# One split pass of 96 rows for the input products of a state-space scan on TensorE

## The chip, the cores and the metric

One core of a Trainium2 chip runs the program. The metric is the device time of one execution in microseconds; the profile is of one execution and counts from its first instruction. TensorE is called PE in the rows, VectorE DVE, ScalarE ACT, GpSimd POOL and SyncE SP.

## The reference

Two blocks follow each other on 256 tokens of width 2048. The first has two layers, each with mixing (two attentions and a gating), attention over a memory, and a gated feed-forward of width 5632. The second block runs once: sliding-window attention beside a state-space branch, both gated, merged and projected. All is float32. What the change touches is the start of the state-space branch. `u` (256 tokens x 1024) is cut into 64 groups of 16 features, and every group has 64 complex states:

```
bu_re = einsum('blgh,gph->blgp', u, B_re)
bu_im = einsum('blgh,gph->blgp', u, B_im)
b_re, b_im = cf * (bu_re + i bu_im)          # a factor per state, folded into C in the kernel
s[t] = a * s[t-1] + b[t]                     # complex, along the 256 tokens
y = einsum(s_re, C_re) - einsum(s_im, C_im) + D_skip * u
```

## The kernel before

**Weights and their split.** All large weights come as one stream of 512 KB units, 1032 in all, two 128-row blocks by 512 columns each. SP loads a unit into one of four slots (L644). ScalarE rounds it to fp32r (`hi`, L1149), VectorE writes the rest (`lo = raw - hi`, L1708), and TensorE multiplies hi by xh, lo by xh and hi by xl (L677 to L679 in form "T", 12 matmuls with 512 columns; L685, L687, L688 in form "C", 24 matmuls with 256 columns). An fp32r matmul takes one pass; the three products together stand for a float32 one. A slot is free when its unit has been multiplied, so the hi split of a unit waits for TensorE to finish the unit four before it, and the splits run three units ahead at most.

**Order of work.** Every engine has one instruction queue, in the order of the code. In the second block that order is one list, `SMIX`, made by `second_steps()`: all units of the weight stream in turn, and between them the other steps, each with a position in units. Every engine walks through the same list and does its own part of each step; ScalarE and VectorE split three units ahead of the unit that the list has reached. So a step at position 28.5 stands on TensorE between units 28 and 29, and on ScalarE between the hi splits of units 31 and 32. In this block u0 and u1 are units 0 to 15, ag0 and ag1 16 to 31, then ga0, ap0, ga1, ap1 and so on; units 80 to 95 (z0, z1) are of form C, as are 0 to 31. Window attention (steps wL, wE, wT, wV) lies at positions 6 to 24.

**The scan.** The 64 groups are worked in 8 chunks (`c`) of 8 groups, that is 128 features and 4 x 128 states. Chunk c begins at position 26.5 + 12.2 c:
- `inputs` re and im (L1074 to L1083, TensorE, positions +0 and +1): four matmuls each, recorded as two instructions a matmul, with a 128x128 block of `bpad` as weights and `uT[:, c, :]` (128 features x 256 tokens) as the moving side, both plain float32, into PSUM. `bpad` holds B of the chunk placed block-diagonally, zeros in between.
- `back` 0 to 5 (L2419 to L2435, VectorE, from +0.6): a rotation that turns the complex recurrence into a real one. back 0 waits for re, back 2 for im.
- `scan` (L2443, VectorE, from +4.2): eight scans of 256 tokens.
- `forward` 0 to 5 (L2452 to L2463, VectorE, from +6.8): the rotation back. After it the states are ready (L2464).
- `outputs` (L1092, TensorE, +11.9): 8 plain float32 matmuls of the states with `cpad`. `skip` (L2475, VectorE, +12.9) adds u.
- `turns` (L1651 to L1664, ScalarE, +12.6 for chunk c + 2): loads of the two rotation tables and of `bpad` for a coming chunk; `maps` (L1587, ScalarE, +14): two loads of `cpad` for the next chunk. For chunks 1 to 6 this position is just after the next chunk's im products.
- `out` ga, gs (L1557, ScalarE): the sigmoid gate of a finished group; where the function changes, a table load goes before it. `silu` (L1610, L1613) is alike.

`bpad` (two buffers) is loaded whole from an array that the host has laid out with its zeros, 512 KB a chunk. `uT` is written by VectorE from the accumulator (L2319). The rotation tables are made in the last feed-forward and stored to DRAM; in the second block ScalarE, VectorE and GpSimd wait once for these stores before they reuse the memory.

The order of one chunk on ScalarE, from the code (L1646 to L1668):

```
elif step == "turns":
    c = at[0]
    if c >= 2:
        act.wait_ge(states, c - 1)
    act.wait_ge(turns_stored[c % 2], 16 * (c // 2 + 1))
    act.dma_start(flat(rotc[c % 2]), ...)
    act.dma_start(flat(rots[c % 2]), ...)
    ...
    else:
        after_turn(act, pos, STP[f"s{c - 2}_im"])
        act.dma_start(flat(bpad[c % 2]), ...)
```

Of the kernel before, what the change touches and what calls it, by code (L numbers as in the profile page):

```python
# [183 lines left out]
def second_steps():  # L184


    steps = [(1, "head_rows"), (5, "head_turns")]
    for k in range(8):
        at = 6 + 2 * k
        steps += [(at, "wL", k), (at + 1, "wE", k), (at + 2, "w_weights", k), (at + 3, "wT", k), (at + 4, "wV", k)]  # L190
    names = ["u0", "u1", "ag0", "ag1"] + [f"{a}{n}" for n in range(4) for a in ("ga", "ap")] + ["z0", "z1"]
    names += ["gs0", "gs1", "gs2", "gs3"]
    at, ends = 0, {}
    for name in names:
        at += SG[name].units
# [82 lines left out]
def build(nc, stream, x, mem, params, rows, post_g, sparams, sinks, onehot, rel, b_pad, c_pack, out,  # L278
          toep_scratch, mem_scratch, turn_scratch, map_scratch):
    ctx = ExitStack()  # L280
    with ctx:
# [84 lines left out]
        assert made_at + 24576 <= place[0] + 4096  # L366
        hTh = at_offset("hTh", qp_at, [P, 4, T], F32R)
# [44 lines left out]
        bpad = [at_offset(f"bpad{n}", r_at + 12288 + 4096 * n, [P, 2, 4, P]) for n in range(2)]  # L412
# [104 lines left out]
        bc_loaded = [sem(f"bc_loaded{n}") for n in range(2)]  # L517
# [136 lines left out]
        def _(pe):  # L654
# [373 lines left out]
            for step, *at in SMIX:  # L1028
# [114 lines left out]
        def _(act):  # L1143
# [169 lines left out]
            for layer in range(L):  # L1313
# [178 lines left out]
                else:  # L1492
                    act.dma_start(craw[:, :, :, :].rearrange("p m s w -> p (m s w)"), c_pack).then_inc(craw_loaded, 16)
                    for j in range(1, NJ):
                        c = j - 2
                        makes = 0 <= c < NCT
                        if makes:
# [13 lines left out]
                        if makes:  # L1511
# [5 lines left out]
                            elif c > 1:  # L1517
# [12 lines left out]
                               .then_inc(turns_stored[c % 2], 16)  # L1530
                        units.ahead(pos, LG[f"up{j}"])
# [29 lines left out]
            for n in range(2):  # L1561
                act.wait_ge(turns_stored[n], 16 * (NCT // 2))
# [27 lines left out]
            for step, *at in SMIX:  # L1590
# [54 lines left out]
                elif step == "turns":  # L1645
# [57 lines left out]
        def _(dve):  # L1703
# [232 lines left out]
            for layer in range(L):  # L1936
# [302 lines left out]
                else:  # L2239
# [17 lines left out]
                    for j in range(1, NJ):  # L2257
# [21 lines left out]
                        across(pos, j - 1)  # L2279
                        gate(pos, j)  # L2280
# [16 lines left out]
            for n in range(2):  # L2297
                dve.wait_ge(turns_stored[n], 16 * (NCT // 2))
# [62 lines left out]
            for step, *at in SMIX:  # L2361
# [20 lines left out]
                elif step == "out":  # L2382
                    name = at[0]
                    n = int(name[-1])
                    if name in ("u0", "u1"):
                        by_rows(name, uT[:, 4 * n:4 * n + 4, :])
                    elif name in ("ag0", "ag1"):
# [5 lines left out]
                    elif name in ("ap0", "ap1", "ap2", "ap3"):  # L2393
# [4 lines left out]
                          .then_inc(acc_read[g.parity], 1)  # L2398
                elif step == "ag_mul":
# [130 lines left out]
        def _(pool):  # L2530
# [128 lines left out]
            for n in range(2):  # L2659
                pool.wait_ge(turns_stored[n], 16 * (NCT // 2))  # L2660
# [101 lines left out]
def input_maps(a):  # L2762

    out = np.zeros((NCT, P, 2, 4, P), np.float32)
    for m, b in enumerate((a["B_re_2"], a["B_im_2"])):
        for g in range(64):
            c, q = g // 8, g % 8
            out[c, 16 * q:16 * q + 16, m, q // 2, 64 * (q % 2):64 * (q % 2) + 64] = b[g].T
    return out.reshape(NCT * P, -1)
# [49 lines left out]
```

## Time and profile before

| | us |
|---|---|
| median of three runs | 3134.56 |
| the three runs | 3132.56 to 3136.55 |
| the profiled execution, its own time | 3131.19 |
| its span, first to last instruction | 3129.5 |

| engine | busy us | share of the span |
|---|---|---|
| PE | 3065.6 | 98% |
| DVE | 2000.7 | 64% |
| ACT | 1512.1 | 48% |
| POOL | 74.9 | 2% |

Busy time counts computing instructions; waits and the issuing of transfers don't count. Matmuls overlap each other, so the duration of a single one is longer than its distance to the next. Rows marked DVEq or ACTq are of an engine's instruction queue: a drain, or the issue of a transfer.

### The profile page before, as it was taken

To read this page: it belongs to the slowest core of one execution; us is meant where nothing else is said; L and a number is where in the kernel's file an instruction comes from. 1 tells how busy PE (TensorE), PEld (TensorE's weight loads), DVE (VectorE), ACT (ScalarE), POOL (GpSimd) and SP (SyncE) were. 2 spreads that over 40 slices of the span, in tenths; PEclk is the share of its full clock that TensorE was granted. 3 is DMA by queue.
4 is the path that set the end of the run, shared out by engine and by line. 5 is a ranking of instruction groups with operands and counts; after the bars stand their busy time and mean duration, and the time that the engine had idled before them with its cause. 6 is when DMAs were issued, how large, how long until landed. Compare 5 with 4: busy or idle time off the path is not lost.

```text
span 3129.5 us, 44692 instructions
## 1 busy us (share of the span) xinstructions
PE 3065.6 (98%) x16254; PEld 2635.3 (84%) x16254; DVE 2000.7 (64%) x2330; ACT 1512.1 (48%) x1972; POOL 74.9 (2%) x124
## 2 busy tenths in 40 slices
PE   9999998999999999999998999999999999999999
PEld 8899787888888888898887888888887898888887
DVE  6467756555555555667756656556656667888664
ACT  6545546444444444645556455555544554334443
POOL 0000000000000000000000000000000200000000
PEclk9999999999999999999999999999999999999999
DMA  7655554655555555554554666666665545555555
GB/s 268 214 177 164 169 175 149 220 192 192 190 187 191 191 189 181 183 170 154 180 171 159 209 217 204 202 214 208 205 204 173 179 140 197 199 200 187 166 183 174
DMA packets 168364, 588.50 MB, mean 188 GB/s; under 512 B 26189, under 2 KB 26377, under 8 KB 165897
## 3 DMA queue, kind: packets, MB, share of 16 engines
q1 hardware_dynamic: 150784, 545.33, 52.9%
q10 hardware_dynamic: 14968, 28.47, 2.6%
q0 software_dynamic: 2464, 12.67, 1.3%
q8 instruction: 101, 1.65, 0.2%
q14 instruction: 47, 0.39, 0.0%
HBM read 572.74 MB, written 13.93 MB: 187 GB/s over the span
## 4 chain that ended last, share of the span: by engine, by line
PE 92%; DVE 4%; ACT 1%; issue 1%; DVEq 1%; DMA 1%; POOL 0%; POOLq 0%; SPq 0%; ACTq 0%
PE acc L677 23%; PE acc L678 23%; PE acc L679 23%; PE acc L685 5%; PE acc L688 5%; PE acc L687 5%; PE tp L723 1%; DVE lo L1708 1%; PE tp L1092 1%; PE tp L1081 1%; PE tp L753 1%; ACT hi L1149 0%; PE tp L868 0%; PE tp L1069 0%; PE tp L1053 0%
## 5 line engine op out<-in xcount | busy, mean ns | idle before, releaser
L1708 DVE TENSOR_TENSOR lo<-raw,hi 128x1024 fp32r<-128x1024 f32 x1032 | 1245.6, 1214 | 843.4 <-ACT hi L1149 833.9
L1149 ACT ACTIVATE hi<-raw 128x1024 fp32r<-128x1024 f32 x1032 | 1079.0, 1050 | 1252.4 <-PE acc L679 1043.5
L677 PE MATMUL acc<-hi,xh 128*128 128x512 f32 (+2 forms) x2512 | 976.8, 389 | 10.4 <-issue 10.1
L679 PE MATMUL acc<-hi,xl 128*128 128x512 f32 (+2 forms) x2512 | 968.0, 385 | 0.0
L678 PE MATMUL acc<-lo,xh 128*128 128x512 f32 (+2 forms) x2512 | 967.5, 385 | 0.0
L677 PEld LDWEIGHTS acc<-hi,xh 128*128 128x128 f32 x2512 | 472.9, 188 | 103.9 <-issue 11.8
L679 PEld LDWEIGHTS acc<-hi,xl 128*128 128x128 f32 x2512 | 472.5, 188 | 94.2
L678 PEld LDWEIGHTS acc<-lo,xh 128*128 128x128 f32 x2512 | 473.0, 188 | 91.0
L685 PE MATMUL acc<-xh,hi 128*128 128x256 f32 x1152 | 332.7, 289 | 3.0 <-issue 2.4
L687 PE MATMUL acc<-xl,hi 128*128 128x256 f32 x1152 | 325.7, 283 | 0.0
L688 PE MATMUL acc<-xh,lo 128*128 128x256 f32 x1152 | 325.7, 283 | 0.0
L677 PE MATMUL acc<-hi,hTh 128*128 128x512 f32 x640 | 249.4, 390 | 1.6 <-DVE lo L1708 1.6
L678 PE MATMUL acc<-lo,hTh 128*128 128x512 f32 x640 | 249.0, 389 | 0.0
L679 PE MATMUL acc<-hi,hTl 128*128 128x512 f32 x640 | 249.0, 389 | 0.0
L685 PEld LDWEIGHTS acc<-xh,hi 128*128 128x128 f32 x1152 | 220.6, 191 | 8.4 <-issue 6.2
L687 PEld LDWEIGHTS acc<-xl,hi 128*128 128x128 f32 x1152 | 220.8, 192 | 0.4
L688 PEld LDWEIGHTS acc<-xh,lo 128*128 128x128 f32 x1152 | 220.6, 191 | 0.0
L677 PEld LDWEIGHTS acc<-hi,hTh 128*128 128x128 f32 x640 | 120.1, 188 | 27.3 <-DVE lo L1708 2.4
L679 PEld LDWEIGHTS acc<-hi,hTl 128*128 128x128 f32 x640 | 120.1, 188 | 25.0
L678 PEld LDWEIGHTS acc<-lo,hTh 128*128 128x128 f32 x640 | 120.1, 188 | 24.8
L2222 DVE TENSOR_TENSOR y<-y,acc 128x1024 f32<-128x1024 f32 x80 | 97.6, 1220 | 36.5 <-PE acc L679 36.5
L2193 DVE TENSOR_TENSOR hTl<-tp,hTh 128x1024 fp32r<-128x1024 f32 x20 | 24.5, 1224 | 51.4 <-ACT hTh L1467 51.4
(406 smaller groups left out, 2615.0 us busy)
## 6 DMA issues: line engine op xcount, KB each, us to landing
raw<-in_stream SPq DMA_DIRECT2D x1032, 512.0 KB, 3.9
turn_scratch<-made ACTq DMA_DIRECT2D x8, 1024.0 KB, 6.8
gpost<-in_post_g POOLq DMA_DIRECT2D x6, 1024.0 KB, 5.1
rotc<-turn_scratch ACTq DMA_DIRECT2D x8, 512.0 KB, 4.8
rots<-turn_scratch ACTq DMA_DIRECT2D x8, 512.0 KB, 6.8
bpad<-in_b_pad ACTq DMA_DIRECT2D x8, 512.0 KB, 8.7
y<-in_mem SPq DMA_DIRECT2D x4, 512.0 KB, 7.9
h<-in_x ACTq DMA_DIRECT2D x4, 512.0 KB, 6.6
```

Source lines behind the costliest of these rows:

```text
L677: nc.tensor.matmul(o, ah, high, start=first, stop=False)
L678: nc.tensor.matmul(o, ah, low, start=False, stop=False)
L679: last = nc.tensor.matmul(o, al, high, start=False, stop=final)
L685: nc.tensor.matmul(o, wh, a_h[:, c, :], start=first and b % 2 == 0, stop=False, skip_group_check=True)
L687: nc.tensor.matmul(o, wh, a_l[:, c, :], start=False, stop=False, skip_group_check=True)
L688: last = nc.tensor.matmul(o, wl, a_h[:, c, :], start=False, stop=final, skip_group_check=True)
L723: last = nc.tensor.transpose(o[:, c, t * P:(t + 1) * P], src, ident[:, :])
L753: last = nc.tensor.transpose(o[:, c, t * P:(t + 1) * P], h[:, t, (4 * q + c) * P:(4 * q + c + 1) * P], ident[:, :])
L1081: last = nc.tensor.matmul(o[:, j, :], bpad[c % 2][:, ("re", "im").index(part), j, :], uT[:, c, :], start=True, stop=True)
L1149: nc.scalar.activation(hi[s][:, :, 0:w], raw[s][:, :, 0:w], ACT.Copy).then_inc(hi_done, 1)
L1708: nc.vector.tensor_tensor(lo[s][:, :, 0:w], raw[s][:, :, 0:w], hi[s][:, :, 0:w].bitcast(F32), ALU.subtract).then_inc(split_done, 1)
L2222: nc.vector.tensor_tensor(y[:, :, n * W:(n + 1) * W], y[:, :, n * W:(n + 1) * W], a[:, :, :], ALU.add).then_inc(acc_read[g.parity], 1)
```

## The change

B and u are each split into a high fp32r part and a low rest, as the streamed weights are. The three partial products are stacked in the row dimension of TensorE: for a block of 32 features (two groups), rows 0 to 31 hold B high and u high, rows 32 to 63 B high and u low, rows 64 to 95 B low and u high. One fp32r matmul of 96 rows replaces one float32 matmul of 128 rows; its number and its 256 columns stay.

- **B's halves.** The host hands over B packed without zeros (`b_rows`, 128 x 1024). In the last step of the last feed-forward (j = 10) ScalarE loads it, rounds it to `b_half[0]`, VectorE makes `b_half[1]`, and ScalarE stores both to DRAM (`b_scratch`). The three waits for the turn stores become waits for these two stores (`b_stored`).
- **u's halves.** For each half of u (n = 0, 1), ScalarE rounds (`u_high`), VectorE subtracts (`u_low`), ScalarE stores both (`u_store`), all in window attention.
- **The stack.** `b_stack` is cleared once by VectorE (`b_zero`, position 23.5). The new step `stack` on ScalarE issues nine transfers a chunk: three of u (32 rows of four pieces of 1 KB) and six of B (16 rows of eight pieces of 256 bytes). There is one buffer of each, so the stack of chunk c + 1 waits for chunk c's im products; it stands at +2, behind `maps`. `bpad` and its loads go away.

```diff
-    steps += [(0, "turns", 0), (24.5, "turns", 1)]
+    steps += [(0, "turns", 0), (23.5, "b_zero"), (24.5, "stack", 0), (24.6, "turns", 1)]
+    for n in range(2):
+        at = ends[f"u{n}"]
+        steps += [(at + 1.6, "u_high", n), (at + 2.6, "u_low", n), (at + (4, 6)[n], "u_store", n)]
...
-            scan += [(14, "maps", c + 1)]
+            scan += [(2, "stack", c + 1), (14, "maps", c + 1)]
...
                     c, part = at
-                    pe.wait_ge(bc_loaded[c % 2], 16 * (c // 2 + 1))
-                    if c == 0:
-                        after_group(pe, pos, SG["u1"])
+                    pe.wait_ge(stack_loaded, 144 * (c + 1))
                     o = take_turn(pe, pos, STP[f"s{c}_{part}"])
                     for j in range(4):
-                        last = nc.tensor.matmul(o[:, j, :], bpad[c % 2][:, ("re", "im").index(part), j, :], uT[:, c, :],
+                        last = nc.tensor.matmul(o[:, j, :], b_stack[:, ("re", "im").index(part), j, :], u_stack[:, j, :],
                                                 start=True, stop=True)
...
+                        if j == NJ - 1:
+                            for n in range(2):
+                                act.wait_ge(turns_stored[n], 16 * (NCT // 2))
+                            act.dma_start(b_raw[:, :], b_rows).then_inc(b_loaded, 16)
...
+                        if j == NJ - 1:
+                            units.before(pos, LG[f"up{j}"], 3, LU + SLOTS)
+                            act.wait_ge(b_loaded, 16)
+                            nc.scalar.activation(b_half[0][:, :], b_raw[:, :], ACT.Copy).then_inc(b_high, 1)
+                            units.before(pos, LG[f"up{j}"], 6, LU + SLOTS)
+                            act.wait_ge(b_high, 1)
+                            act.wait_ge(b_low, 1)
+                            for m in range(2):
+                                act.dma_start(b_scratch[m]..., b_half[m][:, :].bitcast(F32)).then_inc(b_stored, 16)
...
-                    elif c == 1:
-                        for b in range(2):
-                            act.dma_start(flat(bpad[b]), b_pad[b * P:(b + 1) * P, :]).then_inc(bc_loaded[b], 16)
+                elif step == "stack":
+
+                    c = at[0]
+                    if c:
+                        see_turn(act, pos, STP[f"s{c - 1}_im"])
                     else:
-                        after_turn(act, pos, STP[f"s{c - 2}_im"])
-                        act.dma_start(flat(bpad[c % 2]), b_pad[c * P:(c + 1) * P, :]).then_inc(bc_loaded[c % 2], 16)
+                        act.wait_ge(b_clear, 1)
+                    act.wait_ge(u_stored, 32 if c < 4 else 64)
+                    for k, m in enumerate((0, 1, 0)):
+                        act.dma_start(u_stack[32 * k:32 * k + 32, :, :].bitcast(F32),
+                                      u_scratch[m, c, :, :].rearrange("(j r) t -> r j t", r=32)).then_inc(stack_loaded, 16)
+                    for k, m in enumerate((0, 0, 1)):
+                        for q in range(2):
+                            row = 32 * k + 16 * q
+                            act.dma_start(b_stack[row:row + 16, :, :, 64 * q:64 * q + 64].bitcast(F32),
+                                          b_scratch[m, c, q, :, :].rearrange("i (m j s) -> i m j s", m=2, j=4))\
+                               .then_inc(stack_loaded, 16)
+                elif step == "u_high":
+                    n = at[0]
+                    act.wait_ge(u_scaled, n + 1)
+                    if n:
+                        act.wait_ge(u_stored, 32)
+                    nc.scalar.activation(u_half[0][:, :, :], uT[:, 4 * n:4 * n + 4, :], ACT.Copy).then_inc(u_hi, 1)
+                elif step == "u_store":
+                    n = at[0]
+                    act.wait_ge(u_low, n + 1)
+                    for m in range(2):
+                        act.dma_start(u_scratch[m, 4 * n:4 * n + 4, :, :].rearrange("c p t -> p c t"),
+                                      u_half[m][:, :, :].bitcast(F32)).then_inc(u_stored, 16)
...
+                elif step == "b_zero":
+                    nc.vector.memset(flat(b_stack).bitcast(F32), 0.0).then_inc(b_clear, 1)
+                elif step == "u_low":
+                    n = at[0]
+                    dve.wait_ge(u_hi, n + 1)
+                    nc.vector.tensor_tensor(u_half[1][:, :, :], uT[:, 4 * n:4 * n + 4, :], u_half[0][:, :, :].bitcast(F32),
+                                            ALU.subtract).then_inc(u_low, 1)
```

## Rows read from the trace of the kernel before

**Rows 1.** The page: busy time of each engine, share of the span, instructions.
```profile
PE 3065.6 (98%) x16254; PEld 2635.3 (84%) x16254; DVE 2000.7 (64%) x2330; ACT 1512.1 (48%) x1972; POOL 74.9 (2%) x124
```

**Rows 2.** The source line of the input products: duration ns min/median/max, first and last start.
```profile
L1081 PE MATMUL tp<-uT,bpad x128: 377/379/381, 2607.6 to 2899.8; 128*128 128x256 f32 x128
```

**Rows 3.** The chain that ended last: start us, duration us, what.
```profile
2650.19 1.73 PE tp L1081 x8
```

**Rows 4.** The timeline, PE, weight products of form C: start us, us, engine, line, operation.
```profile
2605.73 0.28 PE L688 MATMUL acc<-xh,lo 128*128 128x256 f32 x1
2605.85 0.28 PE L685 MATMUL acc<-xh,hi 128*128 128x256 f32 x1
```

**Rows 5.** Windows, t0 to outputs: us, then busy PE, PEld, DVE, ACT, POOL; PEclk, DMA share, GB/s.
```profile
2609.54:2646.47 36.93, 35.17 (x212) 31.32 (x211) 34.26 (x34) 17.18 (x17) 0.00 (x0) 1.00 0.44 143
2651.92:2686.36 34.44, 34.42 (x152) 28.20 (x151) 30.75 (x31) 14.23 (x14) 0.00 (x0) 1.00 0.57 195
...
2734.41:2766.29 31.88, 31.66 (x140) 25.94 (x139) 30.66 (x31) 11.43 (x13) 0.00 (x0) 1.00 0.51 170
2774.50:2810.16 35.66, 35.66 (x249) 33.55 (x249) 34.05 (x34) 12.26 (x12) 0.00 (x0) 1.00 0.53 171
2815.35:2851.00 35.65, 35.65 (x249) 33.54 (x249) 33.01 (x33) 14.86 (x14) 0.00 (x0) 1.00 0.50 169
2856.19:2890.58 34.39, 34.39 (x153) 28.54 (x153) 30.77 (x32) 14.11 (x14) 0.00 (x0) 1.00 0.55 189
```

**Rows 6.** The timeline, DVE, the last rotation of chunks 1, 4, 5 and 6.
```profile
2685.07 1.22 DVE L2463 TENSOR_TENSOR sd<-sd,sr 128x1024 f32<-128x1024 f32 x1
...
2806.22 1.22 DVE L2463 TENSOR_TENSOR sd<-sd,sr 128x1024 f32<-128x1024 f32 x1
...
2848.63 1.22 DVE L2463 TENSOR_TENSOR sd<-sd,sr 128x1024 f32<-128x1024 f32 x1
...
2888.10 1.22 DVE L2463 TENSOR_TENSOR sd<-sd,sr 128x1024 f32<-128x1024 f32 x1
```

**Rows 7.** The timeline, ACT and its queue, chunk 1; in brackets idle before and releaser.
```profile
2646.45 0.33 ACTq L1651 DMA_DIRECT2D rotc<-turn_scratch  x1
2646.81 0.46 ACTq L1653 DMA_DIRECT2D rots<-turn_scratch  x1
2647.31 0.44 ACTq L1664 DMA_DIRECT2D bpad<-in_b_pad  x1
...
2654.81 0.94 ACTq L1587 DMA_DIRECT2D cpad<-map_scratch  x2
2655.86 1.28 ACT L1557 ACT_TABLE_LOAD   x1
2657.15 1.27 ACT L1557 ACTIVATE sgr<-acc,small 128x512 f32<-128x512 f32 x2
2659.24 1.06 ACT L1149 ACTIVATE hi<-raw 128x1024 fp32r<-128x1024 f32 x1 [0.82 <-PE acc L679]
```

**Rows 8.** The timeline, DVE, low splits of chunks 0, 1 and 5 that waited for a high one.
```profile
2618.20 1.23 DVE L1708 TENSOR_TENSOR lo<-raw,hi 128x1024 fp32r<-128x1024 f32 x1 [1.12 <-ACT hi L1149]
...
2660.33 1.23 DVE L1708 TENSOR_TENSOR lo<-raw,hi 128x1024 fp32r<-128x1024 f32 x1 [2.10 <-ACT hi L1149]
...
2827.33 1.22 DVE L1708 TENSOR_TENSOR lo<-raw,hi 128x1024 fp32r<-128x1024 f32 x1 [0.96 <-ACT hi L1149]
```

**Rows 9.** ACT's queue before chunk 0; then cpad's loads, issue to landing.
```profile
2600.16 1.19 ACTq L1661 DMA_DIRECT2D bpad<-in_b_pad  x2
...
DMA to landing us min/median/max: 2.4/3.4/9.5
```

**Rows 10.** Windows at the start of the second block, columns as in rows 5.
```profile
2424.00:2427.00 3.00, 1.23 (x8) 0.84 (x8) 2.56 (x4) 2.78 (x3) 1.91 (x2) 1.00 0.41 141
2427.00:2430.00 3.00, 1.95 (x9) 1.56 (x9) 1.66 (x4) 1.91 (x6) 0.00 (x0) 0.52 0.00 0
2430.00:2433.00 3.00, 3.00 (x7) 2.38 (x8) 3.00 (x6) 1.12 (x4) 0.00 (x0) 0.50 0.00 0
```

More of the change, by code:

```diff
@@ L275, with build @@
 NQ = 16
-def build(nc, stream, x, mem, params, rows, post_g, sparams, sinks, onehot, rel, b_pad, c_pack, out,
-          toep_scratch, mem_scratch, turn_scratch, map_scratch):
+def build(nc, stream, x, mem, params, rows, post_g, sparams, sinks, onehot, rel, b_rows, c_pack, out,
+          toep_scratch, mem_scratch, turn_scratch, map_scratch, b_scratch, u_scratch):
     ctx = ExitStack()
@@ L366, in build @@
         assert made_at + 24576 <= place[0] + 4096
+        b_raw = at_offset("b_raw", made_at, [P, 8 * P])
+        b_half = [at_offset(f"b_half{n}", made_at + 4096 * (1 + n), [P, 8 * P], F32R) for n in range(2)]
         hTh = at_offset("hTh", qp_at, [P, 4, T], F32R)
@@ L411, in build @@
         st = at_offset("st", r_at + 8192, [P, 4, T])
-        bpad = [at_offset(f"bpad{n}", r_at + 12288 + 4096 * n, [P, 2, 4, P]) for n in range(2)]
+        b_stack = at_offset("b_stack", r_at + 12288, [96, 2, 4, P], F32R)
+        u_stack = at_offset("u_stack", r_at + 16384, [96, 4, T], F32R)
+        u_half = [at_offset(f"u_half{n}", m_at + 16384 + 4096 * n, [P, 4, T], F32R) for n in range(2)]
         zs = at_offset("zs", r_at + 24576, [P, 8, T])
@@ L516, in build @@
         ag_split = sem("ag_split")
-        bc_loaded = [sem(f"bc_loaded{n}") for n in range(2)]
+        b_loaded = sem("b_loaded")
+        b_high = sem("b_high")
+        b_low = sem("b_low")
+        b_stored = sem("b_stored")
+        b_clear = sem("b_clear")
+        u_scaled = sem("u_scaled")
+        u_hi = sem("u_hi")
+        u_low = sem("u_low")
+        u_stored = sem("u_stored")
+        stack_loaded = sem("stack_loaded")
         whole = sem("whole")
@@ L1530, in _ @@
                                .then_inc(turns_stored[c % 2], 16)
+                        if j == NJ - 1:
[6 more added lines that the diff above has]
+                            for m in range(2):
+                                act.dma_start(b_scratch[m].rearrange("c q i w -> (c q i w)").rearrange("(p w) -> p w", p=P),
+                                              b_half[m][:, :].bitcast(F32)).then_inc(b_stored, 16)
                         units.ahead(pos, LG[f"up{j}"])
@@ L1560, in _ @@
             raw_norm(pos, 0, "norm", STP, lambda c: spar[:, SC["norm_w"].start + c:SC["norm_w"].start + c + 1], SG["q0"])
-            for n in range(2):
-                act.wait_ge(turns_stored[n], 16 * (NCT // 2))
+            act.wait_ge(b_stored, 32)
             ahead("q0")
@@ L2279, in _ @@
                         across(pos, j - 1)
+                        if j == NJ - 1:
+                            units.before(pos, LG[f"up{j}"], 4, LU + SLOTS)
+                            dve.wait_ge(b_high, 1)
+                            nc.vector.tensor_tensor(b_half[1][:, :], b_raw[:, :], b_half[0][:, :].bitcast(F32), ALU.subtract)\
+                              .then_inc(b_low, 1)
                         gate(pos, j)
@@ L2296, in _ @@
             nc.vector.tensor_copy(rs_wide2[:, :, :], rs.unsqueeze(2).to_broadcast([P, NT, P])).then_inc(rs_spread, 1)
-            for n in range(2):
-                dve.wait_ge(turns_stored[n], 16 * (NCT // 2))
+            dve.wait_ge(b_stored, 32)
             for m in range(2):
@@ L2386, in _ @@
                         by_rows(name, uT[:, 4 * n:4 * n + 4, :])
+                        dve.drain().then_inc(u_scaled, 1)
                     elif name in ("ag0", "ag1"):
@@ L2658, in _ @@
                                     pattern=[[-1, P]], channel_multiplier=1).then_inc(window_ready, 1)
-            for n in range(2):
-                pool.wait_ge(turns_stored[n], 16 * (NCT // 2))
+            pool.wait_ge(b_stored, 32)
             nc.gpsimd.memset(flat(vpad), 0.0)
@@ L2762, in input_maps @@
 def input_maps(a):
[L2764 to L2769, printed above, removed]
+    out = np.stack([a["B_re_2"], a["B_im_2"]]).reshape(2, NCT, 4, 2, 64, 16)
+    return out.transpose(1, 3, 5, 0, 2, 4).reshape(P, -1)
 def output_maps(a):
@@ L2804 @@
         "rel": a["rel_bias"],
-        "b_pad": input_maps(a),
+        "b_rows": input_maps(a),
         "c_pack": output_maps(a),
@@ L2815 @@
     map_scratch = nc.dram_tensor("map_scratch", (P, 2, 4 * NCT, 32), F32, kind="Internal").ap()
-    build(nc, *ins, out, toep_scratch, mem_scratch, turn_scratch, map_scratch)
+    b_scratch = nc.dram_tensor("b_scratch", (2, NCT, 2, 16, 8 * 64), F32, kind="Internal").ap()
+    u_scratch = nc.dram_tensor("u_scratch", (2, NCT, P, T), F32, kind="Internal").ap()
+    build(nc, *ins, out, toep_scratch, mem_scratch, turn_scratch, map_scratch, b_scratch, u_scratch)
     result = run_bass_kernel_spmd(nc, [arrays], core_ids=[0])
```

## The prediction

> **What bounds the kernel now.** The page first: TensorE is busy for 3065.6 of 3129.5 us [rows 1], so time can only come from work that TensorE no longer does, and only where no other engine then ends the stage. The changed line next: 128 instructions tp<-uT,bpad of plain f32 [rows 2], two for each of 64 matmuls, which makes 16 groups of four matmuls. In the chain of waits a group stands as x8 with 1.73 us [rows 3], 0.43 us a matmul. The weight products of the same 128x256 size, split into fp32r parts, start 0.12 us apart in the timeline [rows 4].
>
> Then the scan stage, chunk by chunk. I count from t0, the end of a chunk's real-part products ("re"). The windows run from t0 to the start of that chunk's output products [rows 5]: 36.93, 34.44, 31.88, 35.66, 35.65 and 34.39 us for chunks 0, 1, 3, 4, 5 and 6; chunk 2 is as chunk 1, chunk 7 as chunk 6. TensorE is idle in them for 1.76 us in chunk 0 and 0.22 in chunk 3, otherwise not. But VectorE is busy for 30.7 us and more of each, and what counts is when its last rotation, the states, is done. In chunk 1 that is 2685.07 + 1.22 = 2686.29 [rows 6], and the outputs start at 2686.36: both engines end together, and in chunks 0 to 3 it is so. In chunk 4 the states are done at 2807.44, 32.9 us after t0, with 2.7 us to spare; in chunk 5 after 34.5 us, 1.1 to spare; in chunk 6 after 33.1 us, 1.2 to spare, and chunk 7 is alike [rows 6]. So a shorter product does not simply shorten a chunk: I need VectorE's own path as well.
>
> **What the change removes.** A group of four falls from 1.73 to 4 x 0.12 = 0.48 us, less 1.25 us; the 96 rows put all three products of the split into one pass, so there are still four matmuls. Sixteen groups: 20.0 us of TensorE. Bounds: nothing (if 96 rows in fp32r cost as f32 does) and 1.73 a group; I take 0.48, the nearest row in type and columns. The re group lies before t0 and its 1.25 us is gained in every chunk, 8 x 1.25 = 10.0. The im group lies inside the window, where VectorE decides.
>
> **VectorE's path.** Its queue in a chunk is: rotate re, skip, wait for a hi half, and so on, one lo split for every unit of TensorE (a unit is 2.72 us: chunk 1's window holds 12 of them and the im group, (34.42 - 1.73) / 12 [rows 5]; 24 x 0.12 = 2.88 where the form is C). The last wait for a hi half is the pivot; after it VectorE runs without a gap to the states. The pivots start 2618.20 - 2609.54 = 8.66 us after t0 in chunk 0, 2660.33 - 2651.92 = 8.4 in chunk 1 and within 0.1 of that in chunks 2, 3, 4, 6 and 7, and 11.98 in chunk 5, a unit later, behind a silu [rows 8]. How far the pivot moves is how far the states move.
>
> **What the change adds on ScalarE.** After the im products ScalarE now issues nine transfers (stack) where one stood, in front of the next hi split. The first issue of three takes 0.36 us to the next (2646.45 to 2646.81), that one 0.50 (to 2647.31), and a pair takes 0.94 [rows 7]; with two turn loads before it a pair took 1.19, so one of it up to 0.73 beside another of 0.46 [rows 9]. I take 0.49 each, nearest to a later one in a row, 4.4 us for nine; the ends are 0.37, 3.3 us, if all were as the first, and 0.73, 6.6 us, if all met a full queue. In chunks 1, 2, 4, 5 and 6 the two map loads (0.94) come just before. The im products end 0.48 us after the first unit, at t0 + 3.2 (3.4 with C units), and a hi takes 1.06:
> chunk 0: 3.4 + 4.4 + 1.1 = 8.9, pivot +0.2.
> Chunk 1: hi of the first unit dispatched at 2.75, maps to 3.7, stack to 8.1, then the table load 1.28 and the gate's 1.27 that are queued behind [rows 7] to 10.65, hi to 11.7: +3.3.
> Chunk 2: the same without the table load, 10.45: +2.05.
> Chunk 3: no maps in front, 8.7: +0.3.
> Chunks 4 and 6: 9.2: +0.8. Chunk 5: 9.4, then table load and silu (2.3) and hi, 12.8: +0.8. Chunk 7 has no stack: 0.
>
> **The sum.** A window is the longer of two: TensorE's own time (the old one less idle, less 1.25) and VectorE's (states before, plus the pivot's move). Chunk 0: 33.9 against 37.1, +0.2. Chunk 1: 33.2 against 37.7, +3.3. Chunk 2: +2.05. Chunk 3: 30.4 against 32.15, +0.3. Chunk 4: 34.4 against 33.7, -1.25. Chunk 5: 34.4 against 35.3, -0.35. Chunk 6: 33.1 against 33.9, -0.5. Chunk 7: 33.1 against 33.2, -1.2. Together +2.55; with the re groups -10.0: **-7.45 us**.
>
> The rest I put at nothing, with its cover. B's halves: one hi-sized and one lo-sized operation (1.06, 1.23) in the last feed-forward, under the lead of three units that the splits have; three issues there likewise. Even in chunk 1 ScalarE is busy for only 14.23 of 34.44 us [rows 5]. u's halves: two such pairs and four stores in the attention stage; uncovered, 2 x (1.06 + 1.23) = 4.6 us at most. Clearing the stack is below one lo, 1.2 us. The first stack is the exposed one: nine issues begin where now two turn loads stand before bpad's pair at 2600.16 [rows 9], 0.36 and 0.50 us earlier, at 2599.3, so the last starts at 2603.2 and lands 3.4 us later (cpad's median, a load in pieces of much the same size [rows 9]) at 2606.6; TensorE asks at 2607.81, 1.73 before chunk 0's t0. Margin 1.2 us, so 0; with cpad's longest, 9.5, a stall of 4.9. The two turn loads of chunk 1 go behind it, with 40 us to their use. The old waits for the turn stores become one for B's stores, which were issued well before the last products of the feed-forward: 0.
>
> The profiled execution took 3131.19 us (span 3129.5); less 7.45 is 3123.7. The median of the three runs lies 3.37 us above it, 3134.56, so the median after is **3127.1 us**.
>
> **Rule against row.** The nine issues cost 4.4 us of ScalarE by the rows, and that is what eats half the gain. The Trainium skill, DMA: Bandwidth & Descriptors, "Issuing engines are not separate DMA queues", calls the sequencer's time to initiate a DMA "usually small relative to the DMA itself". By that rule the pivots stay or come forward, and the sum is the first rival's.
>
> **The rivals.**
> First, issues that cost little (0.37 each, or overlapped by ScalarE's work behind them). With 3.3 us for nine the pivots lie 1.1 us earlier, until TensorE's own time ends chunks 4 to 7: -13. With none at all chunk 1's table load and gate no longer push the pivot out, chunks 0 to 3 end about 1 us earlier than now, and it is -19. For it: nothing that follows in the queue needs the transfers, and an activation handed out before them runs on. Against it: the table load starts only after the second map load ended, 2655.86 after 2654.81 + 0.94 [rows 7]. 3115.5 to 3121.5 us.
> Second, the clock. In my forecast TensorE stands still 3.2, 4.5 and 3.3 us at the first three outputs, which it did not before. The trace has such a place: at 2424:2427 TensorE is busy for 1.23 of 3.0 us, and at 2427:2430 and 2430:2433 its granted clock is 0.52 and 0.50, the 1.2 GHz level [rows 10]. Two such windows lose 3 us of work. One fall gives 3130, two 3133. The Trainium skill, TensorE: Matmul & The Clock Gate, "Why this matters for your kernels", asks for no gaps above about 3 us between bursts of matmuls, and so would have it fall in chunk 1 at least. That comes out at one to three falls, 3130 to 3136 us. Against it: in the scan stage the clock stays at 1.00 through chunk 0's idle 1.76 us [rows 5].
> Third, slower: ScalarE's queue. If nine issues in a row meet a full queue and take the 0.73 us each of the pair's long one, the stack takes 6.6 us, 2.2 more in chunks 0, 1, 2, 3, 5 and 6 and 1.5 more in chunk 4: +14.7 - 7.45 = +7.2, 3141.8 us. From 0.62 us an issue on it ends above the time before. For it the pair at 1.19 [rows 9]; against it the issues in chunk 1, all near 0.46 [rows 7].
> Fourth, the product does not get cheaper: then the re groups give nothing and only the pivots' moves in chunks 0 to 3 stay, +5.9, 3140 us. Nothing speaks for it.
>
> **How the numbers follow.** Forecast, with issue times from 0.42 to 0.58 and a small stall of the first stack, 3121 to 3133: 0.55. First rival 0.15; second 0.13; third 0.12; fourth and unseen stalls 0.05. A measurement can tell about 0.2%, 6.3 us: 3128.3 and 3140.8 are the bounds. The forecast lies just inside faster: 0.30 of its 0.55 there, plus the first rival's 0.15: 0.45. Slower: most of the third, and a late first stack together with a fall of the clock: 0.13. Within: 0.42. The range, 3116 to 3138, takes in most of the first rival, the second, and the lower half of the third.
>
> **What would show it.** Right: L1092's matmuls wait for VectorE's drain in chunks 0 to 3, most (4 to 5 us) in chunk 1; a group of inputs at 0.48 us; nine issues of about 4.4 us before a late hi split; outputs of chunk 4 right after a unit. Wrong: input groups far from 0.48; issues of nine above 5.5 or below 3.5 us; a stall at the first inputs; a granted clock below 1 between 2646 and 2760; lateness in the attention stage.

## The result and the profile after

The changed kernel takes 3138.87 us (median of 20 runs, 3137.29 to 3143.01), the kernel before in the same comparison 3133.14 (20 runs, 3131.19 to 3136.55). The ratio is 1.0019, with a 95% interval of 1.0013 to 1.0025: slower by 5.7 us, a bit less than 0.2%, where 7.5 us less was forecast. The profiled execution took 3139.27 us (span 3137.5, before 3129.5).

The page, busy time of the changed kernel:

```profile
PE 3056.7 (97%) x16190; PEld 2622.0 (84%) x16190; DVE 2005.3 (64%) x2334; ACT 1513.2 (48%) x1975; POOL 74.1 (2%) x124
```

Against [rows 1], TensorE is busy for 8.9 us less and DVE and ACT are the same within 5 us, yet the span is longer: TensorE's share fell from 98 to 97%. What went in is idle time. By the forecast the products save 20 us, and in the first experiment below, with fewer waits and no fall of the clock in the scan, TensorE is busy for 3047.0 us, 18.6 less than before. So half of the saving is hidden here by matmuls that took longer, in part those at a lowered clock (5.41 against 3.72 us a group, below); the rest of the difference is not traced. Groups by line, from the start of the scan:

```profile
L1106 PE MATMUL tp<-sd,cpad 128*128 128x256 f32 x128 | 31.4, 401 | 13.2 <-DVEq L2526 13.2
...
L1095 PE MATMUL tp<-u_stack,b_stack 96*128 96x256 f32 x64 | 11.2, 297 | 0.0
```

L1095 is the input product now: 64 instructions where [rows 2] had 128, and no idle time before them, so in this execution the stacks always landed in time. In the chain of waits a group of four is 0.48 us, as forecast, against 1.73 [rows 3]. The idle time stands before the output products L1106, which wait for VectorE's drain behind the last rotation: 13.2 us, against 2.0 before. The waits of TensorE from the first input products to the end name the rest (us in total, times, longest):

```profile
PE tp L1106 <- DVEq L2526: 13.2, 8, 2.4
PE acc L693 <- DVE lo L1758: 5.9, 9, 1.4
PE acc L701 <- DVE lo L1758: 0.7, 2, 0.4
```

Here are the windows from each chunk's t0 to its outputs, which answer to [rows 5] (columns as there; chunks 0 to 7):

```profile
2610.65:2648.71 38.06, 34.53 (x209) 30.15 (x208) 37.08 (x37) 17.79 (x18) 0.00 (x0) 1.00 0.57 183
2652.91:2692.97 40.06, 34.59 (x149) 26.79 (x148) 31.13 (x32) 14.82 (x15) 0.00 (x0) 1.00 0.58 181
2697.17:2734.82 37.65, 34.41 (x148) 26.81 (x147) 30.67 (x31) 13.66 (x14) 0.00 (x0) 1.00 0.64 194
2741.80:2774.94 33.14, 30.75 (x136) 24.83 (x135) 30.56 (x31) 13.50 (x14) 0.00 (x0) 1.00 0.58 177
2781.90:2818.02 36.12, 35.09 (x245) 32.47 (x243) 31.70 (x32) 13.29 (x14) 0.00 (x0) 1.00 0.54 173
2822.21:2858.99 36.78, 34.42 (x246) 32.18 (x244) 31.98 (x32) 15.13 (x15) 0.00 (x0) 1.00 0.62 194
2864.86:2900.36 35.50, 33.69 (x149) 27.03 (x148) 29.63 (x30) 15.13 (x16) 0.00 (x0) 1.00 0.56 180
2904.56:2937.92 33.36, 33.17 (x148) 27.17 (x147) 29.54 (x30) 17.62 (x18) 0.00 (x0) 1.00 0.54 172
sum 290.67, PE 270.65 PEld 227.43 DVE 252.28 ACT 120.94 POOL 0.00; mean PE 33.83 PEld 28.43 DVE 31.54 ACT 15.12 POOL 0.00
```

Window less PE busy, summed, is 20.0 us of idle; before it was about 2. The windows grew where they should have shrunk: 290.67 us in all against 277.8 before, +12.9, where the forecast had +2.55. Why, chunk 1 on ScalarE and its queue shows (timeline; it answers to [rows 7]):

```profile
2655.75 1.06 ACT L1163 ACTIVATE hi<-raw 128x1024 fp32r<-128x1024 f32 x1 [6.41 <-PE acc L695]
2655.78 0.94 ACTq L1614 DMA_DIRECT2D cpad<-map_scratch  x2
2656.81 1.54 ACTq L1695 DMA_DIRECT2D u_stack<-u_scratch  x3
2658.39 4.57 ACTq L1700 DMA_DIRECT2D b_stack<-b_scratch  x6
2663.04 1.28 ACT L1585 ACT_TABLE_LOAD   x1 [6.23 <-issue]
2664.33 1.27 ACT L1585 ACTIVATE sgr<-acc,small 128x512 f32<-128x512 f32 x2
2665.49 3.90 ACT L1163 ACTIVATE hi<-raw 128x1024 fp32r<-128x1024 f32 x4
```

Nine issues last from 2656.81 to 2662.96, 6.15 us. ScalarE computes nothing for 6.23 us, with "issue" as the releaser, and then does four hi splits without a pause: they had been due. The first low split behind them on VectorE, the pivot, which answers to [rows 8]:

```profile
2666.58 1.22 DVE L1758 TENSOR_TENSOR lo<-raw,hi 128x1024 fp32r<-128x1024 f32 x1 [7.38 <-ACT hi L1163]
...
2691.66 1.22 DVE L2525 TENSOR_TENSOR sd<-sd,sr 128x1024 f32<-128x1024 f32 x1
```

VectorE stood still for 7.38 us, and its last rotation ended at 2692.88, the outputs started at 2692.97. The pivot (the last low split in a window that waits for a high one) lies 13.7 us after t0, where it was 8.4: +5.3, forecast +3.3. In chunks 2 to 6 the pivots moved by 3.3, 1.3, 3.1, 2.2 and 2.3 us and the end of the last rotation by the same to 0.1 us, so the path behind the pivot kept its length; in chunk 7, without a stack, neither moved by more than 0.1.

**Where the 5.7 us come from.** The two spans differ by 8.0 us. The last store of a rotation table was issued at 2305.91 before and at 2308.14 after, and the change's first instruction (the load of B's rows) comes only at 2331.97, so 2.2 us of the 8.0 lie ahead of all that was changed (there the granted clock fell at other places in the two profiles: in the stretch 100 to 120 us it was 0.91 after and 1.00 before). That leaves 5.8, about the difference of the medians. From the first input group to the last outputs it is 327.75 us against 322.34, +5.4: windows +12.9, re groups and the spaces between windows -9.2, and +1.7 for a fall of the clock at one group of outputs:

```profile
2858.99 5.41 PE L1106 MATMUL tp<-sd,cpad 128*128 128x256 f32 x16 [2.36 <-DVEq L2526]
```

The same group takes 3.72 us in the timeline for the other chunks. In the stretch 2858 to 2864.4 the granted clock was 0.73, a mean over the levels of 2.4 and 1.2 GHz.

### The profile page after: what moved, and what is told of

Same layout as the page of the kernel before. It is cut to its first block, busy times and chain, and to the rows that moved or that the text cites. A ratio compares the mean times of both kernels' runs of the same rounds, so it can differ in the third digit from the quotient of the medians.

```text
span 3137.5 us, 44652 instructions
## 1 busy us (share of the span) xinstructions
PE 3056.7 (97%) x16190; PEld 2622.0 (84%) x16190; DVE 2005.3 (64%) x2334; ACT 1513.2 (48%) x1975; POOL 74.1 (2%) x124
## 4 chain that ended last, share of the span: by engine, by line
PE 85%; DVE 7%; DVEq 2%; ACT 2%; issue 1%; ACTq 1%; DMA 1%; POOL 0%; POOLq 0%; SPq 0%
PE acc L693 22%; PE acc L695 22%; PE acc L694 22%; PE acc L701 4%; PE acc L704 4%; PE acc L703 4%; DVE lo L1758 2%; PE tp L739 1%; PE tp L1106 1%; DVE sr L2505 1%; ACT hi L1163 1%; PE tp L769 1%; ACTq L1700 1%; DVEq L2526 1%; DMA raw<-in_stream 1%
## 5 line engine op out<-in xcount | busy, mean ns | idle before, releaser
L2272 DVE TENSOR_TENSOR y<-y,acc 128x1024 f32<-128x1024 f32 x80 | 97.7, 1221 | 36.5 <-PE acc L695 36.5
L2243 DVE TENSOR_TENSOR hTl<-tp,hTh 128x1024 fp32r<-128x1024 f32 x20 | 24.5, 1225 | 51.4 <-ACT hTh L1481 51.4
```

What stands on the lines that cost most here:

```text
L2272: nc.vector.tensor_tensor(y[:, :, n * W:(n + 1) * W], y[:, :, n * W:(n + 1) * W], a[:, :, :], ALU.add).then_inc(acc_read[g.parity], 1)
```

## The experiments

The main theory (Q): the nine issues hold ScalarE's queue in front of the hi split that VectorE's pivot waits for, and VectorE's path sets the outputs. The rivals: the stack's transfers disturb the weight stream or the engines wherever they are issued (T); the added splits of B and u cost it (S); VectorE does not limit, and TensorE's sum is the bound (P). Each series has its own runs of the kernel before, with medians from 3132.4 to 3133.6 us; the ratios are taken against those.

### Does the place of the issues matter?

```diff
# one step for each third: u rows 32k.., and B's two pieces of it
-            scan += [(2, "stack", c + 1), (14, "maps", c + 1)]
+            scan += [(14, "maps", c + 1)]
+            scan += [(6 + k, "stack", c + 1, k) for k in range(3)]
```

> The stack's nine issues are cut into three steps of three, at +6, +7 and +8 of a chunk instead of all at +2; the same transfers, the same bytes. Theory Q (ScalarE's queue holds back the hi split that VectorE's path hangs on): three issues, 1.7 us, fit between two hi splits there, so the hi split after the im products is on time again; every chunk's window from re to outputs ends by TensorE's own time or within 1 us of it: 3114 to 3119 us, some 20 below the changed kernel. Rival T (the small transfers themselves slow the weight stream or the memory): the same transfers are made, 3137 to 3140. Rival S (the added splits and waits before the scan cost the time): 3137 to 3140 as well.

Measured: 3116.88 us (3116.29 to 3118.47), ratio to before 0.9946 (0.9933 to 0.9960).

```diff
-            scan += [(2, "stack", c + 1), (14, "maps", c + 1)]
+            scan += [(7, "stack", c + 1), (14, "maps", c + 1)]
```

> All nine issues in one step, at +7 instead of +2. Theory Q: the block of 5.5 us now falls where VectorE lags behind ScalarE by 3 to 5 us, so most of it is hidden: 3116 to 3124 us; each window 0 to 1 us longer than with three steps. Rivals T and S: 3137 to 3140.

Measured: 3117.20 us (3115.60 to 3118.95), ratio 0.9945 (0.9932 to 0.9959). Waits of TensorE with the thirds, over the scan to the end:

```profile
PE tp L1108 <- DVEq L2528: 4.0, 4, 2.4
PE acc L695 <- DVE lo L1760: 0.9, 2, 0.5
```

The same transfers and the same splits, five units later, take 22 us off, and 16 us against the kernel before. T and S cannot explain that. The waits went from 19.8 to 4.9 us. Both versions beat both kernels. The windows with all nine issues at +7 are 37.81, 33.83, 33.30, 31.23, 34.45, 34.43, 33.16 and 33.36 us, together 271.57, 19.1 less than in the changed kernel: 6.2 of it in chunk 1, 4.4 in chunk 2, 1.7 to 2.4 in each of chunks 3 to 6, but only 0.25 in chunk 0. The clock's fall, 1.7 us, is absent as well. In the timeline of the thirds the three issues now stand beside a hi split that is already under way:

```profile
2666.10 1.06 ACT L1165 ACTIVATE hi<-raw 128x1024 fp32r<-128x1024 f32 x1 [1.66 <-PE acc L697]
2666.18 0.33 ACTq L1697 DMA_DIRECT2D u_stack<-u_scratch  x1
2666.55 1.34 ACTq L1702 DMA_DIRECT2D b_stack<-b_scratch  x2
2668.82 1.06 ACT L1165 ACTIVATE hi<-raw 128x1024 fp32r<-128x1024 f32 x1 [1.66 <-PE acc L697]
```

Each third takes 1.7 us and fits between two hi splits that start 2.72 us apart. The single late block works too. As a reason I take that behind the pivot the splits have a lead to give up; that is argued.

### What is the cheaper product worth?

```diff
+                        ws, us = b_stack[:, ("re", "im").index(part), j, :], u_stack[:, j, :]
+                        if part == "re":
+                            ws, us = ws.bitcast(F32), us.bitcast(F32)
```

> The changed kernel with the real-part products made in plain float32 from the same 96-row stacks (four passes, 1.73 us a group instead of 0.48); the imaginary part stays in one pass. The output stays the three partial products. Theory Q: the re group lies ahead of VectorE's path, so each chunk loses its 1.25 us: +10, 3149 us. Rival P (VectorE does not limit; TensorE's sum is the bound): also +10. If the saving in TensorE had been worth nothing at all: 3139.

Measured: 3149.01 us (3148.18 to 3151.85), ratio 1.0049 (1.0035 to 1.0063): 10.1 above the changed kernel, and 8 x 1.25 is 10.0. The price of the re group, and that all of it lies on the path, are shown. Theory Q and rival P expected the same here, so this run does not tell them apart.

The same edit with `part == "im"`:

> The changed kernel with the imaginary-part products in plain float32, the real part in one pass. Theory Q: the im group lies beside VectorE's path; its only effect is that the stack's issues wait for it, 1.25 us in chunks 0 and 3, about 0.4 in 1, 2, 4, 5 and 6 where the two map loads stand before them, none in chunk 7: +4 to +5, 3143 us. Rival P (TensorE's sum is the bound): +10 as for the real part, 3149.

Measured: 3145.39 us (3143.28 to 3147.28), ratio 1.0035 (1.0023 to 1.0047). The im groups are worth 6.5 us, between the two expectations; rival P's 3149 lies above all six runs. The trace shows two ways in which the im group counts. The stack's issues wait for its end, and counted from t0 the block begins 1.2 us later in chunks 0 and 3 and 0.5 to 0.9 later in chunks 1, 2, 5 and 6. And chunk 7, which has no stack, takes 34.40 us with no idle time of TensorE, where it was 33.36: there TensorE's own time ends the window, which the forecast had and the expectation of this run left out. The windows sum to 295.8 us, 5.1 above the changed kernel; the profile also has two falls of the clock in the scan where the changed kernel's has one.

### How does the time follow the block's length?

Only u's three loads after chunk 0; the reload of B is left out, so that chunks 1 to 7 multiply with chunk 0's B:

```diff
-                    pe.wait_ge(stack_loaded, 144 * (c + 1))
+                    pe.wait_ge(stack_loaded, 144 + 48 * c)
-                    for k, m in enumerate((0, 0, 1)):
+                    for k, m in enumerate((0, 0, 1) if c == 0 else ()):
```

> After chunk 0 only the three loads of u's halves are issued, at the change's place (+2); the six loads of B's pieces are left out, so chunks 1 to 7 use chunk 0's B and the output is not the reference's. Theory Q (the length of the block on ScalarE's queue): three issues take about 1.5 us instead of 5.2 to 6.1, the pivots come back to near their old places, 3114 to 3120 us. Rival T (any change of place or of the semaphores brings the gain, not the number of issues): near the changed kernel, 3135 to 3139.

Measured: 3121.77 us (3119.20 to 3122.72), ratio 0.9962 (0.9949 to 0.9976). That is 1.8 us above theory Q's range and far from rival T's: three issues instead of nine give back 17 us, but before the pivot even three cost some 5 us against none. By the windows 2.1 us of that lie in chunk 1, where the pivot is at 9.5 us after t0 instead of 7.4, and 0.5 in chunk 2; 1.7 more is a fall of the clock at chunk 1's outputs, shown at the end.

All nine, with B's pieces contiguous (2 KB a row, so B's columns are not where the product needs them):

```diff
-   act.dma_start(b_stack[row:row + 16, :, :, 64 * q:64 * q + 64].bitcast(F32),
-                 b_scratch[m, c, q, :, :].rearrange("i (m j s) -> i m j s", m=2, j=4))
+   act.dma_start(flat(b_stack)[row:row + 16, 512 * q:512 * q + 512].bitcast(F32),
+                 b_scratch[m, c, q, :, :])
```

> Nine issues at the change's place, but each of B's six loads writes its rows in one contiguous piece of 2 KB instead of eight pieces of 256 bytes (B lands in the wrong columns, so the output is not the reference's; bytes, rows and count of issues are the same). Theory D (the number of pieces makes an issue of B's 0.62 us): the issues fall to about 0.46 each, 4.3 us for nine, and the time falls by some 1 us a chunk in six chunks, to about 3130 to 3133 us, near what was forecast. Rival N (an issue costs what it costs in a row of nine): 0.6 each and no change, 3137 to 3140.

Measured: 3132.02 us (3129.87 to 3135.09), ratio 0.9998 (0.9989 to 1.0007). The issues of B for chunks 3 and 5 (made in chunks 2 and 4), first in the changed kernel, then here:

```profile
2702.70 3.81 ACTq L1700 DMA_DIRECT2D b_stack<-b_scratch  x6
...
2788.36 3.82 ACTq L1700 DMA_DIRECT2D b_stack<-b_scratch  x6
```

```profile
2703.66 2.89 ACTq L1700 DMA_DIRECT2D b_stack<-b_scratch  x6
...
2788.52 2.81 ACTq L1700 DMA_DIRECT2D b_stack<-b_scratch  x6
```

Same bytes, same rows, same number of issues: 0.64 us each in eight pieces a row, 0.48 each in one. For these loads the pieces a row are the cause, and the 1 us a chunk that they cost is about 7 us of the kernel's time. The count of pieces alone is no price list, though: one of cpad's loads, 128 rows of four pieces of 128 bytes, has four times as many pieces as one of B's and takes 0.47 us. What in the shape of B's loads costs the 0.16 us stays open. The Trainium skill, Perfetto Trace Analysis, "DMA Instruction — HWDGE (DVE, Sync)", says that the sequencer is held until all descriptors of the transfer have been generated; that B's issues get shorter with fewer pieces agrees with it, and cpad's row does not follow from it.

The stack of chunks 1 to 7 issued from GpSimd's queue, at the same moment:

```diff
+            for c in range(1, NCT):
+                pool.wait_ge(tp_full, pos.n("turn", STP[f"s{c - 1}_im"] + 1))
+                pool.wait_ge(u_stored, 32 if c < 4 else 64)
+                for k, m in enumerate((0, 1, 0)):
+                    pool.dma_start(u_stack[32 * k:32 * k + 32, :, :].bitcast(F32), ...)
...
```

> The stack of chunks 1 to 7 is issued from GpSimd's queue, at the same moment (end of the im products), and nothing stands on ScalarE's. Theory Q: ScalarE's hi splits are no longer late; 3112 to 3118 us, a little below the thirds. Rival T (the transfers' traffic, wherever they are issued, holds up the stream or VectorE): 3130 or more. A third way: GpSimd's issues hold up VectorE's operations beside them; then VectorE's busy time rises and it is 3120 to 3130.

Measured: 3117.95 us (3114.74 to 3119.75), ratio 0.9950 (0.9936 to 0.9963). GpSimd's timeline, chunk 1:

```profile
2658.12 1.65 POOL L2733 DMA_DIRECT2D u_stack<-u_scratch  x3 [38.40 <-PE tp L1096]
2659.76 3.15 POOL L2738 DMA_DIRECT2D b_stack<-b_scratch  x6
```

The transfers of chunks 1 to 7 start as early as in the changed kernel and cost nothing that shows: with this T falls a second time, since here their moment was kept. It also settles a row that seems to speak for T. Between 2600 and 2960 us the changed kernel's high splits waited 21 times for a unit of the weight stream, 47.1 us in all, and the kernel before never; with the same transfers on GpSimd it is one wait of 1.7 us. So it was the hold-up on ScalarE that set the stream back, and not the traffic. VectorE's busy time is 2005.7 us, against 2005.3, so the issues on GpSimd do not hold it up either.

The thirds again, but at +2, +3 and +4:

```diff
-            scan += [(2, "stack", c + 1), (14, "maps", c + 1)]
+            scan += [(14, "maps", c + 1)]
+            scan += [(2 + k, "stack", c + 1, k) for k in range(3)]
```

> The stack cut into three steps of three issues as in the thirds at +6, but put at +2, +3 and +4, so before the pivot's hi split, with a hi split of TensorE's next unit between them. Theory Q by the block's place: the same 5.2 to 5.6 us of ScalarE before the pivot, but spread over three units of 2.7 us each, in which ScalarE has about 1 us free beside its other work: the pivot is late by less, 3118 to 3128. Rival (only an unbroken block hurts, because a hi may be up to a slot late): as the thirds, 3115 to 3118. Second rival (all of the issue time before the pivot counts): 3135 to 3139.

Measured: 3122.98 us (3121.11 to 3124.15), ratio 0.9968 (0.9956 to 0.9980). Cutting the block is worth 16 us, putting all pieces behind the pivot another 6. But the last third is no longer before the pivot: in chunk 1 it is issued from 2662.53, behind the start of the pivot's hi split at 2662.35, and in chunk 2 from 2704.53, behind 2702.71. So part of the 16 us is of place and not of the cut. In this run, too, the clock fell once, at chunk 1's outputs.

Summing the issues of the stack that stand before the pivots, from the timelines of chunks 0 to 6:

| stack | its issues before the pivots, us in all | median us |
|---|---|---|
| on GpSimd | 0 | 3117.95 |
| nine at +7 | 0 | 3117.20 |
| u alone, at +2 | 10.9 | 3121.77 |
| nine, B contiguous, at +2 | 32.3 | 3132.02 |
| nine as changed, at +2 | 38.3 | 3138.87 |

From the second row to the third a microsecond of issue costs 0.4, from the third to the fourth 0.5, at the end 1.1: the first part is taken out of slack (chunks 4 to 6 keep their windows in the third row), the rest goes through in full. These slopes are rough: the medians move by a microsecond from series to series, and the profiles hold between none and two falls of the clock in the scan.

### Is more to be had on ScalarE's queue?

```diff
-            scan += [(14, "maps", c + 1)]
+            scan += [(17, "maps", c + 1)]
```

> The thirds at +6, +7 and +8, and the two map loads moved from +14 (+1.8 of the next chunk, before its pivot) to +17 (+4.8, behind it). The queue's theory: chunks 1 to 7 lose another 0.94 us (2.0 where the pair met a full queue) of ScalarE before the pivot, but VectorE ends the window with idle of TensorE in chunks 1 and 3 only (0.69 and 0.78 us in the thirds' trace), so 1 to 1.5 us less than the thirds' 3116.9: 3115 to 3116.5. Rival (VectorE's path there is its own work, not the pivot): 3116.9, no change. Slower, over 3118, if the maps' landing comes late for the outputs or their place collides with the stack's issues.

Measured: 3116.56 us (3116.36 to 3118.61), ratio 0.9947 (0.9933 to 0.9960).

The same, with `turns` moved from +12.6 to +21:

> As the thirds with maps at +17, and the two turn loads of chunk c+2 moved from +12.6 to +21 (+8.8 of the next chunk), so that no transfer at all is issued before the pivot. The queue's theory: the same as with the maps alone or up to 1 us less, 3114.5 to 3116.5. Rival: no change, or slower if two 512 KB loads beside the stack delay the stream.

Measured: 3116.80 us (3114.97 to 3117.78), ratio 0.9946 (0.9932 to 0.9959). Neither differs from the thirds' 3116.88 us by more than its own spread. The queue's theory expected 1 to 1.5 us less and its ranges end at 3116.5; the rival, no change, fits both runs as well. And the maps' move in the kernel before:

> The kernel before, with the two map loads moved from +14 to +17. In it both engines end chunks 1 to 3 together and TensorE has no idle there, so taking 0.94 us from before the pivots gives nothing: 3132.5 to 3134, within 0.1% of before. If it is faster by 1 us or more in each chunk, part of the thirds' gain would be of VectorE's path alone and not of the product.

Measured: 3132.92 us (3130.82 to 3136.30), ratio 1.0000 (0.9991 to 1.0009). With no transfer at all left before the pivots of chunks 1 to 7 (turns at +21) TensorE still waits as with the thirds:

```profile
PE tp L1108 <- DVEq L2528: 3.9, 3, 2.4
PE acc L695 <- DVE lo L1760: 0.8, 2, 0.4
```

What is left lies mostly in chunk 0: 2.4 us of idle before its outputs in every version with the new product. Its stack is issued at 24.5 on ScalarE in all of them, and there it does hold VectorE up. The thirds' low splits just before the first input products:

```profile
2608.81 2.36 DVE L1760 TENSOR_TENSOR lo<-raw,hi 128x1024 fp32r<-128x1024 f32 x2 [5.42 <-ACT hi L1165]
```

VectorE makes up for this standstill inside chunk 0's window, where it is then busy for 37.2 of 37.8 us; before it was 34.3 of 36.9. No run moved the first stack, so what that would give is open. The moves tried here give nothing beyond some 16.5 us. The kernel before gains nothing from moving its map loads (the only transfers moved in it), so the gain of the thirds is put down to the product.

## Why the prediction was wrong

**What held.** The group at 0.48 us. Its gain of 10.0 for the re groups (shown by undoing it, 10.1). The place of the effect: ScalarE's queue, the pivot, VectorE's run to the states, the outputs. The zeros for the halves: in the attention stage TensorE's waits are the same as before, to 0.1 us, so the halves of B and u and the clearing are covered. The first stack was issued from 2601.72 to 2607.19, in 5.5 us where 4.4 were reckoned, and TensorE did not wait for it at 2610.17; but the forecast asked only when it lands, and it costs by another path, told below.

**The step that failed: "I take 0.49 each, nearest to a later one in a row, 4.4 us for nine".** Nine took 5.17, 6.15, 5.44, 5.17, 5.29, 5.63 and 5.44 us in chunks 0 to 6, 0.61 an issue. The rows in hand were issues of other shapes: bpad's, in whole rows, and cpad's pair, in pieces of 128 bytes. I took one price for all nine and treated the piece count of B's loads as known only for the landing. u's loads were priced rightly (0.44 to 0.53 each); B's six are 0.64 to 0.76. The prediction had the break-even at 0.62 us an issue, so at 0.61 its own sum gives about nothing instead of -7.45; the rest of the way to slower came from the terms below. The range to 3138 stopped 0.9 us short.

The windows, forecast against measured, show how much of the miss this term carries. The last column is the window with the nine issues at +7, behind the pivot:

| chunk | forecast | measured | miss | stack over 4.4 us | with the stack at +7 |
|---|---|---|---|---|---|
| 0 | 37.1 | 38.06 | 0.96 | 0.77 | 37.81 |
| 1 | 37.7 | 40.06 | 2.36 | 1.75 | 33.83 |
| 2 | 36.5 | 37.65 | 1.15 | 1.04 | 33.30 |
| 3 | 32.15 | 33.14 | 0.99 | 0.77 | 31.23 |
| 4 | 34.4 | 36.12 | 1.72 | 0.89, and 1.08 from cpad | 34.45 |
| 5 | 35.3 | 36.78 | 1.48 | 1.23 | 34.43 |
| 6 | 33.9 | 35.50 | 1.60 | 1.04 | 33.16 |
| 7 | 33.2 | 33.36 | 0.16 | none | 33.36 |

The misses sum to 10.4 us. In chunks 1 to 6 the stack's excess is 6.7 of it. In chunk 4 cpad's pair took 2.02 us, in [rows 7] it took 0.94; of the two excesses there some 0.7 us went into the slack that the forecast had left for TensorE. The blocks of chunks 1 to 6 also began 0.1 to 0.3 us later after t0 than reckoned, about 1 us in all. Chunk 0's 0.96 is not its own window's stack: behind the pivot that stack takes only 0.25 us off. By the trace it is the first stack, at 24.5; no run moved it. The forecast put it at nothing because it would land in time, and left out that its nine issues stand before due hi splits. On ScalarE, then on VectorE:

```profile
2608.42 2.96 ACT L1163 ACTIVATE hi<-raw 128x1024 fp32r<-128x1024 f32 x3 [5.51 <-issue]
2609.51 2.36 DVE L1758 TENSOR_TENSOR lo<-raw,hi 128x1024 fp32r<-128x1024 f32 x2 [5.35 <-ACT hi L1163]
```

The rotation of chunk 0's re products began 3.6 us after t0, where it was 0.6. With +10.4 the sum is +2.95 instead of -7.45. The re groups and the spaces between windows gave 9.2 instead of 10.0 (+0.8), and the clock 1.7: together +5.4, what the trace shows from first inputs to last outputs. So of the 12.9 us between forecast and trace the price of an issue is about half, and the rest is the first stack, cpad's pair, the later start of the blocks, the re groups and spaces, and the clock, each 0.8 to 1.7. With contiguous pieces, 4.6 us a block, so near the 4.4 of the forecast, the kernel takes 3132.0, still 4.9 us above the forecast. The profile of that run, itself at 3134.59 us, has two falls of the clock, with 0.96 granted over 40 us each: 2 x 0.04 x 40 = 3.2 us. How many the median execution has is not known.

**The rivals.** The first (issues that cost little) is refuted. The third was right in its place, the issues' price on ScalarE's queue, and that price, 0.73 an issue, was about as far above the measured 0.61 as the forecast's 0.49 was below; its reason, a full queue, no run tests, and B's price fell with its pieces a row. The rule weighed there, that initiating a DMA is "usually small relative to the DMA itself" (the Trainium skill, DMA: Bandwidth & Descriptors, "Issuing engines are not separate DMA queues"), speaks of the DMA; here a single issue is indeed 0.61 us against landings of 4.1 to 4.4, and nine of them still decide the sign of the change, because they block a queue. The second rival came true once in this profile, as part of the cause: 1.7 of 13 us. The fourth is refuted.

## What to carry to other kernels

Before transfers are put on the queue of an engine that computes, find the next instruction behind them that somebody waits for, and put them behind it: the same nine issues cost 22 us before the pivot and nothing that shows behind it. Ask this of every block of issues, the first one too, and not only whether its data land in time. Price an issue from a row of the same shape, with as many pieces a row and of like size, and where the break-even lies inside the bounds of a price, treat the sign as open. A stage in which two engines end together gives back what one of them saves, as soon as the edit touches the other one's path.

## What was not expected of the hardware

- The issue of one and the same load takes longer in more pieces a row: 16 rows of eight pieces of 256 bytes 0.64 us, 16 rows of 2 KB 0.48 us. Beside them 32 rows of four pieces of 1 KB take about 0.5 in a row and 0.33 after a pause, and 128 rows of four pieces of 128 bytes 0.47.
- Nine issues on GpSimd took 4.8 us, no more than on ScalarE, with no cost to VectorE.
- TensorE's clock fell after shorter idle than forecast: after 2.36 us in the row above, and, in the kernel with u alone, after 2.07:

```profile
2689.38 5.37 PE L1106 MATMUL tp<-sd,cpad 128*128 128x256 f32 x16 [2.07 <-DVEq L2526]
```

It did not fall at the changed kernel's second outputs, after the same 2.07 us, nor at its first, after 2.40 us:

```profile
2648.71 3.72 PE L1106 MATMUL tp<-sd,cpad 128*128 128x256 f32 x16 [2.40 <-DVEq L2526]
```

The Trainium skill, TensorE: Matmul & The Clock Gate, "Why this matters for your kernels", asks for no idle above about 3 us between bursts; these rows show falls behind less, and not at every such place. What decides between them stays open.
